# State tiles each with its own place, a joint gate product, and first high halves copied by ScalarE

## The chip, the cores and the metric

One core of a Trainium2 chip runs one step of a hybrid decoder layer. The metric is device time in microseconds (us); lower is better. PE is TensorE (matmuls), DVE is VectorE (elementwise work), ACT is ScalarE (activations and copies), SP is SyncE. DMAs are issued here from SP's queue and, in a few places, from ACT's. All five run at once and meet only at semaphores. The program is a sequence of blocks; every block ends with a barrier of all engines.

## The reference, cut to what matters

```python
xn = rmsnorm(h, norm1)                       # 256 prompt tokens and 8x4 sample tokens, 1024 wide
mq, mk, mv, mo, mi, mf, aq, ak, av, ga, gb = split_proj(xn, w_in)
# mi, mf: 4 + 4 gate columns (one input and one forget gate per head)
hA, C, n, m = mlstm_branch(mq, mk, mv, mo, mi + b_igate, mf + b_fgate, m_norm, C0, n0, m0)
hB = combine_groups(...)                     # dilated window attention
u = sigmoid(ga) * (hA @ w_pa) + sigmoid(gb) * (hB @ w_pb)
h = h + u @ w_o
h = h + moe(rmsnorm(h, norm2))               # 32 experts, top 4
h = h + (p @ w_ple) * sigmoid(rmsnorm(h, norm3) @ w_ple_gate)
```

For the sample tokens `mlstm_branch` multiplies the queries by a stored state `C0` of 8 sequences, 4 heads, 256x256 numbers: one tile of 1 MB for each sequence. The result is normalised, multiplied by a gate, and `hA` goes on to the product with `w_pa`.

## The kernel before, in words

**Lead-in (lines 352 to 547).** `h` gets the tokens. ACT and DVE work out the norms, PE transposes the normed rows, and DVE writes them with the norm weights into `xT` (8 slices of 128 rows by 288 tokens); each of the six writes adds one to `s_xT`. PE then makes the gate product, 8 slices for the input gates and 8 for the forget gates, 4 rows each (line 393). Meanwhile DVE splits `xT` into a rounded high half `xhi` and a rest `xlo`, and then the first piece of the projection weight into `whi` and `wlo`, whose end raises `s_lo`. PE waits for both (lines 397 and 399) and starts the projection: 42 weight pieces of 1 MB (`CHUNKS`), each multiplied as high x high, high x low and low x high for the prompt tokens, and unsplit for the 32 sample tokens. Four raw pieces (`NR`) are loaded ahead by SP; a load waits until PE has used the piece before it in its place.

**Attention (lines 584 to 891).** Two blocks that the diff does not touch.

**mLSTM block (lines 944 to 1209).** SP loads the state tiles. There are six places, two in `ct2` and four in `zaflat`; tile 6 and tile 7 go into the places of tiles 0 and 1. The order on SP's queue is written out by hand: six tile loads, then the stores of the prompt state `C_p` for four heads, then

```python
for b in range(6, NB):
    sp.wait_ge(s_cq, b - 5)
    sp.wait_ge(s_ct[b % 4], 16)
    sp.dma_start(ct[b], ...)
for i in range(4):
    sp.wait_ge(s_cq, 3 + i)
    sp.dma_start(wa[:, 2 * i:2 * i + 2, :], ...)      # w_pa, over the four places in zaflat
```

where `s_cq` counts the tiles that PE has multiplied, and last the small stores `n_s`, `m_p`, `m_s` and a wait for all stores (lines 970 to 972). PE works through four heads, then multiplies the eight tiles into one bank (line 1051), then transposes the finished prompt heads (line 1063, four groups of four, two banks), then the sample head (line 1068). DVE normalises the sample head when all eight tiles are in (line 1193 to `finish`, line 1124), then writes the four transposed groups into `hAT` (line 1199; `hAT` is `xT`), then scales the sample head with ACT's help (lines 1107, 1109, 1202 to 1205) and writes its transposes (line 1208).

**Merge block (lines 1297 to 1561).** SP loads `w_pb`, router weights and expert biases; ACT's queue loads the eight state tiles a second time, into `ring`. PE makes `hA @ w_pa` (line 1286) and, in between, every third step, a state update product (line 1340). DVE prepares the keys of a tile (line 1469), waits for the tile's load, adds the products (line 1474), and SP stores the tile (line 1309). DVE prepares tile b+1 only after tile b. Then DVE splits the expert biases and multiplies the gates (line 1485); PE's second set of products waits for the first of these. Line 1499 adds the branch output to `h`. After that come the experts (line 1575 on) and the last products.

Of the kernel before, what the change touches and what calls it, by code (L numbers as in the profile page):

```python
# [27 lines left out]
F32 = mybir.dt.float32  # L28
F32R = mybir.dt.float32r
# [109 lines left out]
def lay_out(x):  # L139

    x = {k: np.ascontiguousarray(v) for k, v in x.items()}
    a = {k: x[k] for k in ("x_prompt", "x_sample", "cache_k0", "cache_v0", "cache_k1", "cache_v1", "cache_k2",
                           "cache_v2", "w_in", "w_pa", "w_pb", "w_o", "w1", "w2", "w_ple",
                           "w_ple_gate", "norm_f", "b_router")}
    a["ca_in"], a["cb_in"] = CA, CB
    col = lambda v: v.reshape(-1, P).T
    pairs = lambda v: v.reshape(KT // 2, P, 2).transpose(1, 0, 2).reshape(P, KT)
    a["norm_cols"] = np.concatenate([col(x["norm1"][0]), col(x["m_norm"][0]), pairs(x["norm2"][0]), col(x["norm3"][0]),
                                     col(x["norm2"][0])], 1)
    a["w_gates"] = x["w_in"][0][:, GATE0:GATE0 + 2 * MH].reshape(KT, P, 2 * MH).transpose(1, 0, 2)  # L150
    a["b_gates"] = np.stack([x["b_igate"][0], x["b_fgate"][0]], 1)
    a["b1"] = np.tile(x["b1"].reshape(E, 2, 2, 512).transpose(2, 0, 1, 3).reshape(2 * E, 2 * 512), (2, 1))
    a["b2"] = np.tile(x["b2"].reshape(E, 2, 512).transpose(1, 0, 2).reshape(2 * E, 512), (2, 1))
    a["w_router"] = x["w_router"][0].reshape(KT, P, E).transpose(1, 0, 2)
    a["p_prompt"], a["p_sample"] = x["p_prompt"][0, 0], x["p_sample"][0].reshape(NS, PLE)

    C = x["state_C"][0].transpose(1, 0, 3, 2).reshape(MH, NB, 2, P, MD)
    a["CT"] = C.transpose(3, 0, 1, 2, 4)
    n = x["state_n"][0].transpose(1, 0, 2)
    a["n_rows"] = n.reshape(MH * NB, MD)  # L160
    a["n_tok"] = np.repeat(n.reshape(MH * NB, MD), NT, 0)
    a["m_rows"] = x["state_m"][0].T

# [33 lines left out]
def layer(nc, x_prompt, x_sample, cache_k0, cache_v0, cache_k1, cache_v1, cache_k2, cache_v2, w_in, w_pa, w_pb,  # L197
# [68 lines left out]
    def shift_piece(eng):  # L266
# [36 lines left out]
    wlo = sb(st, "wlo", [P, NW, CHUNK], F32R)  # L303
    xhi = sb(st, "xhi", [P, KT, TOK], F32R)
    xlo = sb(st, "xlo", [P, KT, TOK], F32R)
    wif = sb(st, "wif", [P, KT, 2 * MH])
    bif = sb(st, "bif", [MH, 2])
    xn = zaflat[:, 0:3 * D].rearrange("p (t n) -> p t n", t=3)
# [11 lines left out]
    s_lo, s_free, s_xs = sem(st, "s_wlow"), sem(st, "s_wfree"), sem(st, "s_xsplit")  # L320
    s_small = sem(st, "s_small")
    s_ss, s_ms, s_rt, s_xn, s_tr, s_xT = (sem(st, n) for n in (
        "s_sumsq", "s_meansq", "s_root", "s_xn", "s_xtrans", "s_xT"))
# [28 lines left out]
    with nc.Block() as block:  # L352
# [24 lines left out]
        def _(pe):  # L377
# [12 lines left out]
            pe.wait_ge(s_small, 48)  # L390
            for c in range(2):
                for k in range(KT):
                    last = pe.matmul(psG[0:MH, c, 0:TOK], wif[:, k, c * MH:(c + 1) * MH], xT[:, k, :],
                                     start=(k == 0), stop=(k == KT - 1))
                last.then_inc(s_gp, 1)

            pe.wait_ge(s_xs, 2)
            for n, (i, z0, w, k0, nk) in enumerate(CHUNKS):
# [45 lines left out]
        def _(act):  # L444
            for t in range(3):
# [5 lines left out]
                act.wait_ge(s_ms, t + 1)  # L451
                act.activation(ss[0:R, t:t + 1], ss[0:R, t:t + 1], ACT.Sqrt).then_inc(s_rt, 1)
            def stores():
                nb = 4 + 9
# [30 lines left out]
        def _(dve):  # L485
# [17 lines left out]

            high_x, low_x = split(dve, xT[:, :, :], xhi[:, :, :], xlo[:, :, :])
            dve.wait_ge(s_xT, 6)
            high_x().then_inc(s_xs, 1)
            dve.wait_ge(s_xs, 1)
            low_x().then_inc(s_xs, 1)

            def prepare(n):  # L510
                high_w, low_w = split(dve, wraw[:, n % NR, :], whi[:, n % NW, :], wlo[:, n % NW, :])
                dve.wait_ge(s_w[n % NR], 16 * (n // NR + 1))
                if n >= NW:
                    multiplied(dve, n - NW)
                link(high_w())
                low_w().then_inc(s_lo, 1)
# [19 lines left out]
            for n in range(AHEAD):  # L536
                prepare(n)
            for c in range(2):
                dve.wait_ge(s_gp, c + 1)
                dve.tensor_scalar(grow[:, c, :], psG[0:MH, c, 0:TOK], bif[:, c:c + 1], None, ALU.add)  # L540
            dve.wait_ge(s_c, 16)
# [197 lines left out]
    with nc.Block() as block:  # L739
# [72 lines left out]
        def _(dve):  # L812
# [93 lines left out]
    ct2 = sb(ap, "ct", [P, 2, MH, 2 * MD])  # L906
    ct = [(ct2[:, b % 6] if b % 6 < 2 else zaflat[:, (b - 2) * MH * 2 * MD:(b - 1) * MH * 2 * MD].rearrange("p (h n) -> p h n", h=MH))
          for b in range(NB)]
    sv = sb(ap, "sv", [P, MD + 1])
# [34 lines left out]
    with nc.Block() as block:  # L944
        @block.sync
        def _(sp):
            sp.dma_start(nrow[:, :], n_rows).then_inc(s_ld, 16)
            sp.dma_start(ntok[:, :], n_tok).then_inc(s_ld, 16)
            sp.wait_ge(s_stored, n_stored[0])
            for b in range(6):  # L950
                if b >= 4:
                    sp.wait_ge(s_ct[b % 4], 16)
                sp.dma_start(ct[b], CT[:, :, b].rearrange("p h k v -> p h (k v)")).then_inc(s_ct[b % 4], 16)
            for hd in range(MH):
                sp.wait_ge(s_co, 2 * hd + 2)
                sp.dma_start(C_p[hd].rearrange("(a p) e -> p a e", p=P), cst[:, hd % 2].rearrange("p (a e) -> p a e", a=2)).then_inc(s_cst[hd % 2], 16)
                sp.dma_start(n_p[hd:hd + 1], nst[:, hd % 2]).then_inc(s_cst[hd % 2], 16)
            for b in range(6, NB):
                sp.wait_ge(s_cq, b - 5)
                sp.wait_ge(s_ct[b % 4], 16)  # L960
                sp.dma_start(ct[b], CT[:, :, b].rearrange("p h k v -> p h (k v)")).then_inc(s_ct[b % 4], 16)
            for i in range(4):
                sp.wait_ge(s_cq, 3 + i)
                sp.dma_start(wa[:, 2 * i:2 * i + 2, :],
# [10 lines left out]
        def _(pe):  # L975
# [70 lines left out]
            pe.wait_ge(s_qmm, 3)  # L1046
            for b in range(NB):
                pe.wait_ge(s_ct[b % 4], 16 * (b // 4 + 1))
                for half in range(2):
                    for j in range(MH):  # L1050
                        last = pe.matmul(psN_[32 * j:32 * j + 32, 1, 0:MD], qmm[:, half, b, 32 * j:32 * j + 32],
                                         ct[b][:, j, half * MD:(half + 1) * MD],
                                         start=(b == 0 and half == 0), stop=(b == NB - 1 and half == 1))
                last.then_inc(s_cq, 1)

            pe.wait_ge(s_ha, 8)
            for n in range(4):
                if n >= 2:
                    pe.wait_ge(s_hae, n - 1)
                t, half = n // 2, n % 2  # L1060
                for q in range(4):
                    k = 4 * half + q
                    last = pe.transpose(psTR[:, n % 2, q * P:(q + 1) * P], zm[:, t, 2, k * P:(k + 1) * P], ident)
                last.then_inc(s_hat, 1)
            pe.wait_ge(s_ha, 9)
# [46 lines left out]
        def _(dve):  # L1112
# [78 lines left out]
            link(dve.scalar_tensor_tensor(out=sm1[:, 3:4], in0=sm1[:, 2:3], scalar=SC_(3), in1=psN_[:, 0, MD:MD + 1], op0=ALU.mult, op1=ALU.add))  # L1191
            dve.wait_ge(s_cq, NB)
            link(dve.tensor_scalar(ntok[:, :], psN_[:, 1, 0:MD], SC_(3), None, ALU.mult))
            link(dve.tensor_tensor(ntok[:, :], ntok[:, :], psN_[:, 0, 0:MD], ALU.add))
            finish(ntok[:, :], sm1[:, 3:4], SC_(1), zw[:, 3, :])
            for n in range(4):
                dve.wait_ge(s_hat, n + 1)
                t, half = n // 2, n % 2
                dve.tensor_tensor(hAT[:, 4 * half:4 * half + 4, t * P:(t + 1) * P], psTR[:, n % 2, :].rearrange("p (q n) -> p q n", q=4),
                                  mnc[:, 4 * half:4 * half + 4].unsqueeze(2).to_broadcast([P, 4, P]), ALU.mult).then_inc(s_hae, 1)  # L1200
            dve.wait_ge(s_sq, 9)
            dve.tensor_scalar(ssq[:, 8:9], ssq[:, 8:9], 1.0 / MD, EPS, ALU.mult, ALU.add).then_inc(s_sqd, 1)
# [94 lines left out]
    with nc.Block() as block:  # L1297
        @block.sync
        def _(sp):
            vpb = w_pb[0].rearrange("(k p) n -> p k n", p=P)  # L1300
            sp.dma_start(wb_[:, :, :], vpb[:, 0:3, :]).then_inc(s_wb, 16)
            sp.dma_start(ple1[:, :], vpb[:, 3, :]).then_inc(s_wb, 16)
            sp.dma_start(wr[:, :, :], w_router).then_inc(s_sm, 16)
            sp.dma_start(brb, b_router[0].partition_broadcast(P)).then_inc(s_sm, 16)
# [155 lines left out]
        def _(dve):  # L1460
# [29 lines left out]
            def turned(t):  # L1490
                for half in range(2):
# [3 lines left out]
                                      n2r[:, 4 * half:4 * half + 4].unsqueeze(2).to_broadcast([P, 4, ROWS[t]]), ALU.mult).then_inc(s_x2e, 1)  # L1495

            for t in range(2):
                dve.wait_ge(s_pa, 7 + t)
# [546 lines left out]
```

## Time and profile before

| | |
|---|---|
| time, three runs | 1648.76 us median, 1647.61 to 1649.33 |
| the profiled execution | 1647.51 us, of which 1645.7 us are the span from first to last instruction |
| mean granted clock of TensorE | 0.961 of full |
| PE busy | 1500.4 us (91%) |
| DVE busy | 652.7 us (40%) |
| ACT busy | 212.9 us (13%) |
| DMA | 583.00 MB, mean 354 GB/s |

A timeline row reads: start, length, engine, line, operation, tile written <- tiles read, shapes, count, and in brackets how long the engine stood idle before it and what ended that. PEld is the load of a weight into PE, which runs beside products. Matmuls are pipelined: a row of one can overlap the next. An fp32 matmul shows as two records.

### The profile page before, as it was taken

Reading aid. Unit: us, or ns where it says so; the run is one execution under the profiler, and the core shown is the slowest. Engines: PE = TensorE matmul, PEld = TensorE weight load, DVE = VectorE, ACT = ScalarE, POOL = GpSimd, SP = SyncE. Lnnn points to the kernel's source line nnn. Section 1 sums busy time; section 2 is a strip of 40 time slices with the busy share of each in tenths; the row PEclk is TensorE's granted clock in tenths of the full one; section 3 lists DMA queues with packets and bytes.
Section 4 is the critical chain, followed back from the end, with each engine's and each line's share of the span. In section 5 each row is a group of like instructions: output and inputs, shape, how many; then the busy total and the mean of one; then the engine's idle time right before and its main releaser. Section 6 shows DMA issues by size and latency. Waiting matters only on the chain. (4 is left out here: it accounts for less than half of the span.)

```text
span 1645.7 us, 20148 instructions
## 1 busy us (share of the span) xinstructions
PE 1500.4 (91%) x8077; PEld 713.3 (43%) x8077; DVE 652.7 (40%) x1051; ACT 212.9 (13%) x387; POOL 0.3 (0%) x5
## 2 busy tenths in 40 slices
PE   6999999865686898999999999999999999999977
PEld 4777777651463444333333333333333333333333
DVE  5555565345143614133333333333333333323343
ACT  1111110231020002011110111111011111101122
POOL 0000000000000000000000000000000000000000
PEclk9999999987787998999999999999999999999988
DMA  4888889599656993799999999999999999999950
GB/s 167 303 306 306 307 308 364 240 308 415 260 180 237 399 402 142 309 383 428 428 429 428 428 428 429 428 428 428 429 428 428 428 429 428 428 428 429 428 237 29
DMA packets 70200, 583.00 MB, mean 354 GB/s; under 512 B 6116, under 2 KB 8520, under 8 KB 42376
## 3 DMA queue, kind: packets, MB, share of 16 engines
q1 hardware_dynamic: 63528, 570.90, 85.0%
q10 hardware_dynamic: 6624, 11.41, 1.8%
q8 instruction: 37, 0.61, 0.2%
q14 instruction: 11, 0.09, 0.0%
HBM read 568.62 MB, written 67.80 MB: 387 GB/s over the span
## 5 line engine op out<-in xcount | busy, mean ns | idle before, releaser
L1661 PE MATMUL eG<-ring,hBT 128*64 128x512 f32 x1008 | 262.6, 599 | 2.6 <-DMA ring<-w 2.6
L1661 PE MATMUL eL<-ring,hBT 128*64 128x512 f32 x1008 | 259.0, 592 | 0.0
L1703 PE MATMUL eY<-ring,hBT 128*64 128x512 f32 x1024 | 233.9, 598 | 22.0 <-ACT hBT L1743 22.0
L1812 DVE SCALAR_TENSOR_TENSOR h<-eS,rgg,h 128x512 f32<-128x512 f32 (+1 forms) x192 | 135.0, 743 | 208.8 <-PE eS L1687 205.0
L1785 DVE TENSOR_SCALAR xT<-eG 128x512 f32<-128x512 f32 x32 | 22.1, 692 | 302.6 <-PE eL L1661 302.6
L410 PE MATMUL psT<-whi,xhi 128*128 128x512 f32 x336 | 137.0, 408 | 1.2 <-ACT zg L478 1.2
L1661 PEld LDWEIGHTS eL<-ring,hBT 128*64 128x64 f32 x1008 | 72.4, 137 | 143.9 <-issue 143.9
L410 PE MATMUL psT<-whi,xlo 128*128 128x512 f32 x336 | 132.4, 394 | 0.0
L410 PE MATMUL psT<-wlo,xhi 128*128 128x512 f32 x336 | 132.2, 393 | 0.0
L1703 PEld LDWEIGHTS eY<-ring,hBT 128*64 128x64 f32 x1024 | 67.9, 136 | 144.5 <-issue 114.9
L1661 PEld LDWEIGHTS eG<-ring,hBT 128*64 128x64 f32 x1008 | 66.0, 136 | 130.3 <-issue 119.4
L349 DVE CAST whi<-wraw 128x2048 fp32r<-128x2048 f32 x42 | 51.5, 1226 | 122.4 <-PE psT L414 122.4
L350 DVE TENSOR_TENSOR wlo<-wraw,whi 128x2048 fp32r<-128x2048 f32 x42 | 96.3, 2292 | 1.4
L1637 PE MATMUL eA<-zg,selU 128*64 128x512 f32 x396 | 90.6, 592 | 1.7 <-DVE selU L1774 1.7
L1752 ACT ACTIVATE xT<-xT 128x512 f32<-128x512 f32 x32 | 20.2, 630 | 468.3 <-DVE xT L1785 468.3
L410 PEld LDWEIGHTS psT<-whi,xhi 128*128 128x128 f32 x336 | 63.0, 188 | 27.5 <-issue 14.7
L1687 PE MATMUL eS<-yS,selT 128*128 128x512 f32 x192 | 71.5, 452 | 3.7 <-DVE yS L1798 2.7
L410 PEld LDWEIGHTS psT<-whi,xlo 128*128 128x128 f32 x336 | 63.1, 188 | 15.1
L410 PEld LDWEIGHTS psT<-wlo,xhi 128*128 128x128 f32 x336 | 63.2, 188 | 13.1
L1687 PEld LDWEIGHTS eS<-yS,selT 128*128 128x128 f32 x192 | 29.0, 189 | 81.2 <-issue 75.5
L1286 PE MATMUL pX<-za,xT 128*128 128x512 f32 x128 | 61.4, 632 | 2.6 <-PEq L944 2.6
L1637 PEld LDWEIGHTS eA<-zg,selU 128*64 128x64 f32 x396 | 28.4, 137 | 58.1 <-issue 56.0
(411 smaller groups left out, 1279.3 us busy)
## 6 DMA issues: line engine op xcount, KB each, us to landing
ring<-w SPq DMA_DIRECT2D x190, 2048.0 KB, 19.3
wraw<-w_in SPq DMA_DIRECT2D x42, 1024.0 KB, 7.2
k_s<-cache_k SPq DMA_DIRECT2D x8, 2040.0 KB, 10.4
v_s<-cache_v SPq DMA_DIRECT2D x8, 2040.0 KB, 31.6
ring<-CT ACTq DMA_DIRECT2D x8, 1024.0 KB, 17.9
C_s<-ring SPq DMA_DIRECT2D x8, 1024.0 KB, 10.7
k_s<-cache_k SPq DMA_DIRECT2D x4, 2032.0 KB, 9.9
v_s<-cache_v SPq DMA_DIRECT2D x4, 2032.0 KB, 9.9
```

The source lines that it names most:

```text
L349: return (lambda: dve.tensor_copy(high, raw), lambda: dve.tensor_tensor(low, raw, high.bitcast(F32), ALU.subtract))
L350: lambda: dve.tensor_tensor(low, raw, high.bitcast(F32), ALU.subtract))
L410: last = pe.matmul(ps[:, c, :], a[:, k0 + k, t * P:(t + 1) * P], b[:, k, c * 512:(c + 1) * 512], start=(k0 + k == 0 and a is xh and b is w ...
L1286: last = pe.matmul(pX[t][:, c, :], xt[:, k, t * P:(t + 1) * P], wts[k][:, c * 512:(c + 1) * 512], start=(k == 0), stop=(k == kt - 1))
L1637: last = pe.matmul(pA[64 * c:64 * c + 64, :], selU[:, t, 0:CAP], x2[:, t, c * 512:(c + 1) * 512], start=(t == 0), stop=(t == 2))
L1661: last = pe.matmul(ps[64 * hh:64 * hh + 64, :], xgT[:, k % 4, (k // 4) * CAP:(k // 4 + 1) * CAP], src[:, c, col:col + 512], start=False, s ...
L1687: pe.matmul(pSc[c][:, :], selT[:, t * P:(t + 1) * P], yS[:, c, :], start=True, stop=True).then_inc(S["sc"], 1)
L1703: last = pe.matmul(pY[64 * hh:64 * hh + 64, :], acT[:, k % 4, (k // 4) * CAP:(k // 4 + 1) * CAP], ring[:, c, col:col + 512], start=False, ...
L1752: act.activation(sg, glu, ACT.Sigmoid, scale=ALPHA).then_inc(S["sg"], 1)
L1785: dve.tensor_scalar(glu, pG[:, :], LIMIT, None, ALU.min).then_inc(S["glu"], 1)
L1812: dve.scalar_tensor_tensor(out=x, in0=pSc[c][0:R, :], scalar=rgg[0:R, t:t + 1], in1=x, op0=ALU.mult, op1=ALU.add).then_inc(S["acc"], 1)
```

## The change

Three things are changed.

The lead-in: the input gate's 4 columns and the forget gate's 4 columns are laid out in one weight of 36 columns (4, 28 zeros, 4), so that one product of 8 slices gives both, in rows 0 to 3 and 32 to 35 of one bank. ACT copies the first weight piece's high half and, in two pieces of 128 tokens, the high half of `xT`; DVE makes the rests, also in two pieces, for the 256 prompt tokens alone. PE waits for four of these steps.

The mLSTM block: all eight state tiles have a place of their own. Tile 6 lies in `xT` and tile 7 in `h`. They are loaded and multiplied in the order `CQ`, the four of `zaflat` first; no tile load waits for PE any more. The `w_pa` loads wait for the first to the fourth tile multiplied. PE transposes the prompt heads in two parts between the tiles, after the fifth and after the seventh, and DVE writes them out before it normalises the sample head.

The merge block: `h` is loaded again from `x_prompt` (two loads of 512 KB on SP's queue, behind `w_pb`), and DVE waits for it before line 1499.

```diff
-    a["w_gates"] = x["w_in"][0][:, GATE0:GATE0 + 2 * MH].reshape(KT, P, 2 * MH).transpose(1, 0, 2)
+    wg = x["w_in"][0][:, GATE0:GATE0 + 2 * MH].reshape(KT, P, 2 * MH).transpose(1, 0, 2)
+    a["w_gates"] = np.concatenate([wg[:, :, 0:MH], np.zeros((P, KT, 32 - MH), np.float32), wg[:, :, MH:2 * MH]], 2)
...
-    xhi = sb(st, "xhi", [P, KT, TOK], F32R)
-    xlo = sb(st, "xlo", [P, KT, TOK], F32R)
+    xhi = sb(st, "xhi", [P, KT, SEQ], F32R)
+    xlo = sb(st, "xlo", [P, KT, SEQ], F32R)
+    GC = 32 + MH
...
-            for c in range(2):
-                for k in range(KT):
-                    last = pe.matmul(psG[0:MH, c, 0:TOK], wif[:, k, c * MH:(c + 1) * MH], xT[:, k, :],
-                                     start=(k == 0), stop=(k == KT - 1))
-                last.then_inc(s_gp, 1)
-
-            pe.wait_ge(s_xs, 2)
+            for k in range(KT):
+                last = pe.matmul(psG[0:GC, 0, 0:TOK], wif[:, k, :], xT[:, k, :], start=(k == 0), stop=(k == KT - 1))
+            last.then_inc(s_gp, 1)
+
+            pe.wait_ge(s_xs, 4)
...
+            act.wait_ge(s_w[0], 16)
+            act.activation(whi[:, 0, :], wraw[:, 0, :], ACT.Copy).then_inc(s_whi0, 1)
+            for t in range(2):
+                act.wait_ge(s_xT, 2 * t + 2)
+                act.activation(xhi[:, :, t * P:(t + 1) * P], xT[:, :, t * P:(t + 1) * P], ACT.Copy).then_inc(s_xs, 1)
...
-            high_x, low_x = split(dve, xT[:, :, :], xhi[:, :, :], xlo[:, :, :])
-            dve.wait_ge(s_xT, 6)
-            high_x().then_inc(s_xs, 1)
-            dve.wait_ge(s_xs, 1)
-            low_x().then_inc(s_xs, 1)
+            dve.wait_ge(s_xs, 2)
+            for t in range(2):
+                a = slice(t * P, (t + 1) * P)
+                dve.tensor_tensor(xlo[:, :, a], xT[:, :, a], xhi[:, :, a].bitcast(F32), ALU.subtract).then_inc(s_xs, 1)
...
-                link(high_w())
+                if n:
+                    link(high_w())
+                else:
+                    dve.wait_ge(s_whi0, 1)
                 low_w().then_inc(s_lo, 1)
...
+    ct = ([ct2[:, 0], ct2[:, 1]]
+          + [state_rows(zaflat[:, i * MH * 2 * MD:(i + 1) * MH * 2 * MD]) for i in range(4)]
+          + [state_rows(xT[:, :, :].rearrange("p k n -> p (k n)")[:, 0:MH * 2 * MD]),
+             state_rows(h[:, 0:2, :].rearrange("p t n -> p (t n)"))])
+    CQ = (2, 3, 4, 5, 6, 0, 1, 7)
...
-            for b in range(6):
-                if b >= 4:
-                    sp.wait_ge(s_ct[b % 4], 16)
-                sp.dma_start(ct[b], CT[:, :, b].rearrange("p h k v -> p h (k v)")).then_inc(s_ct[b % 4], 16)
+            for i, b in enumerate(CQ):
+                if i >= 4:
+                    sp.wait_ge(s_ct[i % 4], 16)
+                sp.dma_start(ct[b], CT[:, :, b].rearrange("p h k v -> p h (k v)")).then_inc(s_ct[i % 4], 16)
...
-            for b in range(6, NB):
-                sp.wait_ge(s_cq, b - 5)
-                sp.wait_ge(s_ct[b % 4], 16)
-                sp.dma_start(ct[b], CT[:, :, b].rearrange("p h k v -> p h (k v)")).then_inc(s_ct[b % 4], 16)
             for i in range(4):
-                sp.wait_ge(s_cq, 3 + i)
+                sp.wait_ge(s_cq, 1 + i)
...
+            def ha_trans(t):
+                pe.wait_ge(s_ha, 8)
+                for half in range(2):
+                    if t:
+                        pe.wait_ge(s_hae, half + 1)
+                    for q in range(4):
+                        k = 4 * half + q
+                        last = pe.transpose(psTR[:, half, q * P:(q + 1) * P], zm[:, t, 2, k * P:(k + 1) * P], ident)
+                    last.then_inc(s_hat, 1)
+
+            for i, b in enumerate(CQ):
+                pe.wait_ge(s_ct[i % 4], 16 * (i // 4 + 1))
...
                 last.then_inc(s_cq, 1)
-
-            pe.wait_ge(s_ha, 8)
-            for n in range(4):
...
+                if b in (6, 1):
+                    ha_trans(0 if b == 6 else 1)
...
-            dve.wait_ge(s_cq, NB)
-            link(dve.tensor_scalar(ntok[:, :], psN_[:, 1, 0:MD], SC_(3), None, ALU.mult))
-            link(dve.tensor_tensor(ntok[:, :], ntok[:, :], psN_[:, 0, 0:MD], ALU.add))
-            finish(ntok[:, :], sm1[:, 3:4], SC_(1), zw[:, 3, :])
+            dve.wait_ge(s_cq, 5)
             for n in range(4):
                 dve.wait_ge(s_hat, n + 1)
...
+            dve.wait_ge(s_cq, NB)
+            link(dve.tensor_scalar(ntok[:, :], psN_[:, 1, 0:MD], SC_(3), None, ALU.mult))
+            link(dve.tensor_tensor(ntok[:, :], ntok[:, :], psN_[:, 0, 0:MD], ALU.add))
+            finish(ntok[:, :], sm1[:, 3:4], SC_(1), zw[:, 3, :])
...
             sp.dma_start(ple1[:, :], vpb[:, 3, :]).then_inc(s_wb, 16)
+            for t in range(2):
+                sp.dma_start(h[:, t, :], x_prompt[0, t * P:(t + 1) * P]).then_inc(s_hload, 16)
             sp.dma_start(wr[:, :, :], w_router).then_inc(s_sm, 16)
...
+            dve.wait_ge(s_hload, 80)
             for t in range(2):
                 dve.wait_ge(s_pa, 7 + t)
```

## Rows read from the trace of the kernel before

**Rows 1.** The page's slices: busy tenths of PE and of DMA in 40 parts.
```profile
PE   6999999865686898999999999999999999999977
...
DMA  4888889599656993799999999999999999999950
```

**Rows 2.** Timeline of the lead-in, SP's queue, PE and DVE.
```profile
4.02 38.04 SPq L366 DMA_DIRECT2D wraw<-w_in  x6
...
17.88 10.22 PE L393 MATMUL psG<-xT,wif 128*4 128x288 f32 x32 [0.38 <-DVE xT L499]
...
19.25 2.56 DVE L350 TENSOR_TENSOR xlo<-xT,xhi 128x2304 fp32r<-128x2304 f32 x1
...
22.60 0.09 PEld L393 LDWEIGHTS psG<-xT,wif 128*4 128x4 f32 x1 [0.32 <-issue]
...
22.98 2.29 DVE L350 TENSOR_TENSOR wlo<-wraw,whi 128x2048 fp32r<-128x2048 f32 x1
...
27.45 0.09 PEld L393 LDWEIGHTS psG<-xT,wif 128*4 128x4 f32 x1 [0.16 <-issue]
...
28.03 0.50 PE L410 MATMUL psT<-whi,xhi 128*128 128x512 f32 x1
```

**Rows 3.** Timeline of ACT: its first work after the norms.
```profile
51.43 1.03 ACT L478 ACTIVATE zm<-psT 128x1024 f32<-128x1024 f32 x1 [39.00 <-PE psT L410]
```

**Rows 4.** The five weight loads of line 366 that start before 40 us.
```profile
DMA to landing us min/median/max: 4.9/8.6/12.7
```

**Rows 5.** Timeline of PE: state tiles, head transposes, start of the merge block.
```profile
500.65 3.46 PE L1051 MATMUL mN<-ct,qmm 128*32 128x256 f32 x28
...
503.95 3.83 PE L1051 MATMUL mN<-za,qmm 128*32 128x256 f32 x61
...
513.13 1.07 PE L1051 MATMUL mN<-ct,qmm 128*32 128x256 f32 x16 [3.07 <-DMA ct<-CT]
514.13 1.97 PE L1063 MATMUL mTR<-ca,zm 128*128 128x128 f32 x8
...
523.99 7.24 PE L1286 MATMUL pX<-za,xT 128*128 128x512 f32 x12 [2.57 <-PEq L944]
```

**Rows 6.** Timeline of DVE: the sample head and the block's last write.
```profile
514.34 0.48 DVE L1193 TENSOR_SCALAR ntok<-mN,colsb 128x256 f32<-128x256 f32 x1 [9.90 <-PE mN L1051]
...
519.71 0.14 DVE L1202 TENSOR_SCALAR ssq<-ssq 128x1 f32<-128x1 f32 x1
...
521.24 0.51 DVE L1208 TENSOR_TENSOR xT<-mTR,cols 128x128 f32<-128x128 f32 x2 [0.57 <-PE mTR L1068]
```

**Rows 7.** Timeline of ACT beside them: the end of the sample head's square.
```profile
516.79 0.19 ACT L1107 ACTIVATION_READ_ACCUMULATOR scr<-zw 128x1 f32 x1
```

**Rows 8.** Timeline of SP's queue: the two late tile loads.
```profile
503.06 1.89 SPq L961 DMA_DIRECT2D ct<-CT  x2
```

**Rows 9.** SP's waits: total us, times, longest.
```profile
SPq L972 <- DMA m_s<-mnew: 13.2, 1, 13.2
```

**Rows 10.** Windows: PE, PEld, DVE, ACT, POOL busy, granted clock, DMA share, GB/s.
```profile
516.00:518.00 2.00, 1.00 (x5) 0.91 (x5) 1.64 (x3) 0.51 (x2) 0.00 (x0) 0.50 1.04 424
...
540.00:542.00 2.00, 2.00 (x10) 0.83 (x5) 1.19 (x2) 0.00 (x0) 0.00 (x0) 0.50 1.05 389
```

**Rows 11.** Timeline of DVE in the merge block.
```profile
535.59 1.41 DVE L1474 SCALAR_TENSOR_TENSOR ring<-ring,za,pT_ 128x512 f32<-128x512 f32 x2 [11.25 <-DMA ring<-CT]
...
568.59 1.41 DVE L1474 SCALAR_TENSOR_TENSOR ring<-ring,za,pT_ 128x512 f32<-128x512 f32 x2 [1.80 <-DMA ring<-CT]
...
574.39 2.36 DVE L1485 TENSOR_TENSOR zg<-pX,zg 128x1024 f32<-128x1024 f32 x2
```

**Rows 12.** Timeline of PE in the merge block.
```profile
538.63 0.80 PE L1340 MATMUL pT_<-za,ring 32*128 32x256 f32 x2 [3.54 <-DVE ring L1469]
...
540.68 4.87 PE L1286 MATMUL pX<-za,xT 128*128 128x512 f32 x6
...
576.03 2.84 PE L1286 MATMUL pX<-wb,hBT 128*128 128x512 f32 x6
```

More of the change, by code:

```diff
@@ L149, in lay_out @@
                                      col(x["norm2"][0])], 1)
-    a["w_gates"] = x["w_in"][0][:, GATE0:GATE0 + 2 * MH].reshape(KT, P, 2 * MH).transpose(1, 0, 2)
-    a["b_gates"] = np.stack([x["b_igate"][0], x["b_fgate"][0]], 1)
+    wg = x["w_in"][0][:, GATE0:GATE0 + 2 * MH].reshape(KT, P, 2 * MH).transpose(1, 0, 2)
+    a["w_gates"] = np.concatenate([wg[:, :, 0:MH], np.zeros((P, KT, 32 - MH), np.float32), wg[:, :, MH:2 * MH]], 2)
+    a["b_gates"] = np.concatenate([x["b_igate"][0], np.zeros(32 - MH, np.float32), x["b_fgate"][0]])[:, None]
     a["b1"] = np.tile(x["b1"].reshape(E, 2, 2, 512).transpose(2, 0, 1, 3).reshape(2 * E, 2 * 512), (2, 1))
@@ L303, in layer @@
     wlo = sb(st, "wlo", [P, NW, CHUNK], F32R)
-    xhi = sb(st, "xhi", [P, KT, TOK], F32R)
-    xlo = sb(st, "xlo", [P, KT, TOK], F32R)
-    wif = sb(st, "wif", [P, KT, 2 * MH])
-    bif = sb(st, "bif", [MH, 2])
+    xhi = sb(st, "xhi", [P, KT, SEQ], F32R)
+    xlo = sb(st, "xlo", [P, KT, SEQ], F32R)
+    GC = 32 + MH
+    wif = zaw[:, :, :].rearrange("p a b -> p (a b)")[:, 0:KT * GC].rearrange("p (k c) -> p k c", k=KT)
+    bif = sb(st, "bif", [GC, 1])
     xn = zaflat[:, 0:3 * D].rearrange("p (t n) -> p t n", t=3)
@@ L321, in layer @@
     s_small = sem(st, "s_small")
+    s_whi0 = sem(st, "s_whi_first")
     s_ss, s_ms, s_rt, s_xn, s_tr, s_xT = (sem(st, n) for n in (
@@ L537, in _ @@
                 prepare(n)
+            dve.wait_ge(s_gp, 1)
             for c in range(2):
-                dve.wait_ge(s_gp, c + 1)
-                dve.tensor_scalar(grow[:, c, :], psG[0:MH, c, 0:TOK], bif[:, c:c + 1], None, ALU.add)
+                dve.tensor_scalar(grow[:, c, :], psG[32 * c:32 * c + MH, 0, 0:TOK], bif[32 * c:32 * c + MH, :], None, ALU.add)
             dve.wait_ge(s_c, 16)
@@ L906, in layer @@
     ct2 = sb(ap, "ct", [P, 2, MH, 2 * MD])
-    ct = [(ct2[:, b % 6] if b % 6 < 2 else zaflat[:, (b - 2) * MH * 2 * MD:(b - 1) * MH * 2 * MD].rearrange("p (h n) -> p h n", h=MH))
-          for b in range(NB)]
+    state_rows = lambda x: x.rearrange("p (h n) -> p h n", h=MH)
+    ct = ([ct2[:, 0], ct2[:, 1]]
[3 more added lines that the diff above has]
+    CQ = (2, 3, 4, 5, 6, 0, 1, 7)
     sv = sb(ap, "sv", [P, MD + 1])
@@ L1046, in _ @@
             pe.wait_ge(s_qmm, 3)
-            for b in range(NB):
-                pe.wait_ge(s_ct[b % 4], 16 * (b // 4 + 1))
+            def ha_trans(t):
[9 more added lines that the diff above has]
+                pe.wait_ge(s_ct[i % 4], 16 * (i // 4 + 1))
                 for half in range(2):
@@ L1052, in _ @@
                                          ct[b][:, j, half * MD:(half + 1) * MD],
-                                         start=(b == 0 and half == 0), stop=(b == NB - 1 and half == 1))
+                                         start=(i == 0 and half == 0), stop=(i == NB - 1 and half == 1))
                 last.then_inc(s_cq, 1)
-            pe.wait_ge(s_ha, 8)
-            for n in range(4):
[L1058 to L1064, printed above, removed]
+                if b in (6, 1):
+                    ha_trans(0 if b == 6 else 1)
             pe.wait_ge(s_ha, 9)
```

## The prediction

> **What bounds the kernel now.** First the page's slices: PE is at 9 tenths nearly everywhere, and the dips lie in slice 0, in slices 8 to 13 (counted from 0) and at the end [rows 1]. So a gain must come from a place where PE waits or does needless work on the path. The change touches three. The timeline of the lead-in shows that the projection starts at 28.03, directly behind the last gate record at 27.45, while DVE had finished its part at 22.98 + 2.29 = 25.27 [rows 2]: the gate product sets that start, DVE has 2.8 us in hand. In the mLSTM block the timeline of PE shows the eighth tile delayed by 3.07 us by its load, and behind it a row of steps, PE to DVE to ACT and back, up to DVE's write at 521.24 + 0.51 = 521.75 [rows 5, 6]. Yet the next block starts only at 523.99 [rows 5]: SP's waits show 13.2 us for the last small store [rows 9], which stands behind 4 MB of w_pa on SP's queue. So two things end that block almost together, the engines first, SP last. In the merge block DMA is at 9 (slice 13, from 535) [rows 1], and the DVE timeline has two waits for tile loads, 11.25 us for the first and 1.80 us for the last [rows 11].
>
> **Lead-in.** Removed: 8 of 16 gate matmuls, 16 of 32 records. The start of the last 21 records is spaced (27.45 - 22.60)/20 = 0.24 us; the eleven before them take (22.60 - 17.88)/11 = 0.43 each, about twice as long [rows 2]. The new product has the same 288 moving columns, so I take the same time for a record, and 36 instead of 4 weight columns at nothing, as PEld runs beside PE. If the spacing changes at the same time as before, the last of 16 records starts at 22.60 + 4 x 0.24 = 23.57, and with the 0.58 us from the last record to the first projection matmul the projection starts at 24.15: 3.9 us earlier. If all 16 kept the slow spacing: 17.88 + 15 x 0.43 + 0.58 = 24.9, a gain of 3.1.
>
> Does the other input come in time? ACT has stood idle since 51.43 - 39.00 = 12.43 [rows 3]. Weight piece 0 is first of four on one queue, so its load takes no longer than the median 8.6 us of [rows 4], and it was issued at 4.02 [rows 2]: there by 12.6. ACT needs 1.03 us for 1024 elements [rows 3], so about 2.1 for the piece, done by 14.7, and twice 1.03 for xhi. The second of these waits only for the fourth write of xT, which lies before the sixth at about 17.85 (the gate product starts on it), so xhi is complete by 18.9 at the latest. DVE then makes xlo, 2.56 x 2048/2304 = 2.3, plus some 0.1 for the second instruction, and wlo, 2.29 [rows 2]: 23.6 at the latest. That is still 0.5 before 24.15. If the cover failed, each us that ACT is later costs one. Gone from DVE are 1.36 us of xhi and 1.2 of the first high half, both of which were hidden. The most to be had is where DVE sets the start, 17.9 + 2.3 + 2.3 = 22.5, and the gate records are all fast: a gain of 5.2 with a margin for the waits. I take 3.9. The projection after it runs on PE alone (its slices are at 8 and 9), so this passes on whole. The gate additions on DVE, two as before, and the second piece's split stand behind it with a whole piece on PE to hide in.
>
> **mLSTM block.** The tile loads: eight are issued in one run, at the pace of landing, while PE is at the heads; 2 MB more in a stretch whose DMA slice, 11, stands at 5 [rows 1]. I cost them at nothing: PE's heads hide them, and the two last have no wait for PE any more. They go past the four C_p stores on SP's queue; the store of head 0 can be held until the fourth tile has landed, and ACT needs its buffer back only two heads later. If that cover failed, ACT would stand.
>
> On PE the first 32 records (two tiles) ran until 503.95, and the next 64, four tiles, took 3.83 us or 0.96 each [rows 5]. Five tiles then end at 503.95 + 2.87 = 506.8; the first eight head transposes took 1.97, and the window behind them has a granted clock of 0.50, 1.2 GHz [rows 5, 10]; I take half of 1.97, 1.0, because they now follow tiles at the faster pace without a wait: 507.8; two tiles, 509.7; eight transposes, 510.7; the last tile, 1.07: 511.8, where it was 514.2. DVE's four writes of hAT fall between the tiles (PE needs the first two of them 1.9 us after it made their input). The sample head starts 0.14 after the last tile as before: 511.95. To the end of ACT's square with its accumulator it is 516.79 + 0.19 - 514.34 = 2.64 [rows 6, 7]; line 1202, which stood behind the four writes until 519.71, can then follow 0.05 later, and from its start to the last write it is 521.75 - 519.71 = 2.04 [rows 6]. End of the engines: 511.95 + 2.64 + 0.05 + 2.04 = 516.7, 5.1 us earlier.
>
> SP, which was later, must gain too. Before, its queue moved 2 tiles and w_pa, 6.3 MB, from 503.06 [rows 8]; at 424 GB/s [rows 10] that is 14.8 us, and SP was free at about 523.5: 5.6 us went for the start, gaps and the last store's return. Now w_pa alone, 4.2 MB or 9.9 us, is issued from the end of the first tile, about 502.2. With the same 5.6 SP is free at 517.7; if the gaps came from the tile loads, nearer 516. So the block ends between 516.7 and 517.7, and the next starts 0.5 after, between 517.2 and 518.2: 5.8 to 6.8 us earlier. I take 6.3.
>
> **Merge block.** Added: 1.05 MB for h, at 389 to 424 GB/s 2.5 to 2.7 us of all DMA engines, in a stretch whose DMA is full [rows 1, 10]. Who waits? The last tile's load already holds DVE by 1.80, its four additions, two of them 1.41, end near 571.3, the biases follow, the gate product starts at 574.39 and ends its first half at 575.6, and PE's second set of products starts at 576.03 on it [rows 11, 12]. So about 0.4 us of delay is hidden and the rest passes on. From below the cost is nothing (if ACT's queue keeps its share of the engines while SP's is only longer), from above 2.7. The DVE's wait for the last tile shows that its landing counts, so I go above the middle: a delay of 2.1, a cost of 1.7. The wait on h itself (line 1499) comes only after the products with w_o and costs nothing.
>
> The page "DMA: Bandwidth & Descriptors" of the Trainium skill, section "Queues, rings and completion order", says that each DMA engine takes turns between the queues that have work, a packet at a time; that the first tile took over 11 us agrees with shared engines. By that rule the loads of h also slow the first tiles, and the sum would be that of the third rival below.
>
> Sum: 3.9 + 6.3 - 1.7 = 8.5 us. The profiled execution took 1647.51, so 1639.0; the median of the three runs stands 1.25 above it, so **1640.3** for the median. About 0.2%, 3.3 us, is what can be told from no change.
>
> **Rivals.** (1) SP's stores still set the end of the mLSTM block: w_pa lands no faster, for instance because it is held by its own gates, and only 503.06 - 502.2 = 0.9 is won there. For it: SP was last before. Against: a third of the bytes ahead of it are gone. 3.9 + 0.9 - 1.7 = 3.1: 1645.7.
>
> (2) The lead-in gains nothing, as ACT's chain replaces the gate product: then 4.6 in all, 1644.2. It takes a weight piece that lands after about 16, against the bound of 12.6.
>
> (3) h delays the first tile too, by its full 2.5, and PE's wait of 3.54 grows by that; six products behind a wait took 4.87 where they take 2.84 later [rows 12]; one more such round is 2.0. 3.9 + 6.3 - 4.5 = 5.7: 1643.1. Against: the first tile landed while SP's queue still held other loads, so it may not feel a longer queue.
>
> (4) Slower: the clock. After that wait of 3.54 the granted clock was again 0.50 [rows 10], and the six products of a round cost 4.87 - 2.84 = 2.0 us more; its state product took 540.68 - 538.63 = 2.05, and if that is halved at full clock the round costs 3.0 more. If late tiles bring PE into such a wait in every round, the block loses up to 7 x 3.0 = 21 us; from the fourth round on (10.2/3.0 = 3.4) the gain is gone. At five rounds: 1648.76 - 10.2 + 15.0 = 1653.6. Against it: a slow round lasts longer than the loads of a tile, so the loads catch up and the waits end. The page "TensorE: Matmul & The Clock Gate", section "HAM oscillation — how this bites in real kernels", of the Trainium skill tells of just that, a PE put back to the low clock by each wait for a load; the row after the wait agrees once.
>
> **How the numbers follow.** The forecast has 0.70, (1) 0.06, (2) 0.05, (3) 0.15, (4) 0.04. The forecast's own range: gains of 3.1 + 5.8 - 2.7 = 6.2 to 5.2 + 6.8 - 0 = 12.0, so 1636.8 to 1642.6, and the runs spread about 0.9 to either side. The range takes in (3) and (2): 1636.0 to 1645.0. Faster: the forecast, (2) and (3), 0.90; the same: (1), 0.06; slower: (4), 0.04.
>
> **What would show it.** Right: 16 records of line 393, the first projection matmul near 24.2 behind a gate record; the eighth tile without a wait for a load, the merge block's start some 10 us earlier than 523.99 on the profile's clock (3.9 + 6.3); a longer DVE wait at line 1474. Wrong: a projection start released by DVE or ACT; SP in line 972 well after DVE's last write; PE waits of several us in more than two rounds; or a wait for hload.

## The result and the profile after

The changed kernel took 1637.03 us (median of four runs, 1636.32 to 1639.47) where the kernel before took 1648.18 beside it: a ratio of 0.9936, 95% interval 0.9912 to 0.996, so 6.6 to 14.5 us less. The forecast was 1640.3 in a range of 1636.0 to 1645.0. The profiled execution took 1636.94 us, 1635.2 of them the span, at a mean granted clock of 0.965.

The timeline of the lead-in (start, length, engine, line, operation) answers to [rows 2, 3]:

```profile
12.54 1.89 ACT L455 ACTIVATE whi<-wraw 128x2048 fp32r<-128x2048 f32 x1
...
14.82 1.06 ACT L458 ACTIVATE xhi<-xT 128x1024 fp32r<-128x1024 f32 x1 [0.39 <-DVE xT L506]
...
17.04 1.06 ACT L458 ACTIVATE xhi<-xT 128x1024 fp32r<-128x1024 f32 x1 [1.16 <-DVE xT L506]
...
18.08 6.25 PE L395 MATMUL psG<-xT,zaw 128*36 128x288 f32 x16 [0.39 <-DVE xT L506]
18.13 2.36 DVE L514 TENSOR_TENSOR xlo<-xT,xhi 128x1024 fp32r<-128x1024 f32 x2
20.41 2.28 DVE L353 TENSOR_TENSOR wlo<-wraw,whi 128x2048 fp32r<-128x2048 f32 x1
24.26 0.50 PE L411 MATMUL psT<-whi,xhi 128*128 128x512 f32 x1
```

There are 16 gate records instead of 32, and DVE is done at 20.41 + 2.28 = 22.69, 1.6 us before the projection starts. So the gate product still sets that start. From the first gate record to the first projection matmul it is 24.26 - 18.08 = 6.18 us, where it was 28.03 - 17.88 = 10.15 [rows 2]: 4.0 us gained.

The mLSTM block's end, in the timelines of PE and DVE and the waits of SP, answers to [rows 5, 6, 9]. PE:

```profile
494.12 0.65 PE L1070 MATMUL mN<-za,qmm 128*32 128x256 f32 x3
...
500.38 1.09 PE L1063 MATMUL mTR<-ca,zm 128*128 128x128 f32 x8
501.40 1.93 PE L1070 MATMUL mN<-ct,qmm 128*32 128x256 f32 x32
503.26 1.09 PE L1063 MATMUL mTR<-ca,zm 128*128 128x128 f32 x8
504.28 1.07 PE L1070 MATMUL mN<-h,qmm 128*32 128x256 f32 x16
509.13 0.44 PE L1079 MATMUL mTR<-ca,zw 128*128 128x128 f32 x2 [3.77 <-DVE zw L1217]
511.90 1.19 PE L1298 MATMUL pX<-za,xT 128*128 128x512 f32 x1 [2.33 <-PEq L957]
```

DVE, and SP's waits (total us, times, longest):

```profile
509.50 0.49 DVE L1220 TENSOR_TENSOR xT<-mTR,cols 128x128 f32<-128x128 f32 x2 [0.42 <-PE mTR L1079]
511.90 0.35 DVE L1483 TENSOR_SCALAR ring<-za 128x256 f32<-128x256 f32 x1 [1.92 <-PEq L957]
525.32 1.41 DVE L1488 SCALAR_TENSOR_TENSOR ring<-ring,za,pT_ 128x512 f32<-128x512 f32 x2 [13.06 <-DMA ring<-CT]
```
```profile
SPq L981 <- DMA m_s<-mnew: 10.0, 1, 10.0
```

No tile waits for a load any more. From the first state product to the merge block's first product it is 511.90 - 494.12 = 17.78 us. Before, the first state product was this row of PE's timeline, the first of the 32 records of [rows 5]:

```profile
500.23 0.65 PE L1051 MATMUL mN<-ct,qmm 128*32 128x256 f32 x3
```

So it was 523.99 - 500.23 = 23.76: 6.0 gained. The engines finish at 509.50 + 0.49 = 509.99, the barrier opens 1.9 later, and SP is the one that is late: it has waited 10.0 us for its last small store.

The DVE row at 525.32 answers to [rows 11]: the wait for the first tile of the merge block has grown from 11.25 to 13.06. The eighth tile, in the same timeline:

```profile
559.68 1.41 DVE L1488 SCALAR_TENSOR_TENSOR ring<-ring,za,pT_ 128x512 f32<-128x512 f32 x2 [2.15 <-DMA ring<-CT]
```

Its additions start 559.68 - 511.90 = 47.78 us after the block's start, when its load has landed; before it was 568.59 - 523.99 = 44.60, on the load too [rows 11]. PE's timeline there answers to [rows 12]:

```profile
511.90 8.15 PE L1298 MATMUL pX<-za,xT 128*128 128x512 f32 x12 [2.33 <-PEq L957]
...
528.36 0.81 PE L1354 MATMUL pT_<-za,ring 32*128 32x256 f32 x2 [4.44 <-DVE ring L1483]
...
530.40 4.88 PE L1298 MATMUL pX<-za,xT 128*128 128x512 f32 x6
...
536.30 2.84 PE L1298 MATMUL pX<-za,xT 128*128 128x512 f32 x6
...
566.77 2.84 PE L1298 MATMUL pX<-wb,hBT 128*128 128x512 f32 x6
```

PE's wait is 4.44 instead of 3.54, one round runs slowly (4.88 for six products) and the next is at 2.84 again. From the block's start to the second set of products it is 566.77 - 511.90 = 54.87 us, where it was 576.03 - 523.99 = 52.04: 2.8 lost.

That makes 4.0 + 6.0 - 2.8 = 7.2 us, less than the timed difference of 10.5. One more gain is in a place that the prediction passed over. PE's timeline at the first matmul of the third and of the 35th weight piece, first before, then after:

```profile
41.56 0.50 PE L410 MATMUL psT<-whi,xhi 128*128 128x512 f32 x1
...
258.42 0.50 PE L410 MATMUL psT<-whi,xhi 128*128 128x512 f32 x1
```
```profile
37.63 0.50 PE L411 MATMUL psT<-whi,xhi 128*128 128x512 f32 x1
...
251.69 0.50 PE L411 MATMUL psT<-whi,xhi 128*128 128x512 f32 x1
```

The same 32 pieces take 216.86 us before and 214.06 after. PE waits for nobody in either; each matmul simply starts 0.227 us (median) after the one before it instead of 0.232. Over all 42 pieces that would be 2.80 x 42/32 = 3.7 us, an estimate from these 32.

### The profile page after: what moved, and what is told of

The parts are those of the page before. It is cut to its first block and busy times, and to the rows that moved or that the text cites. A ratio compares the mean times of both kernels' runs of the same rounds, so it can differ in the third digit from the quotient of the medians.

```text
span 1635.2 us, 20121 instructions
## 1 busy us (share of the span) xinstructions
PE 1488.8 (91%) x8061; PEld 710.5 (43%) x8061; DVE 650.2 (40%) x1050; ACT 216.8 (13%) x390; POOL 0.3 (0%) x5
```

## The experiments

The table has for each kernel the time, and four intervals of its profile in us. **Lead-in**: first gate record to first projection matmul. **32 pieces**: start of the third to start of the 35th weight piece. **Block**: first state product to the merge block's first product. **Merge**: from there to the second set of products. Each ratio is to runs of the kernel before made beside that kernel, with medians from 1647.55 to 1648.64.

| kernel | median us | ratio to before (95%) | lead-in | 32 pieces | block | merge |
|---|---|---|---|---|---|---|
| before | 1648.18 | | 10.15 | 216.86 | 23.76 | 52.04 |
| changed | 1637.03 | 0.9936 (0.9912 to 0.996) | 6.18 | 214.06 | 17.78 | 54.87 |
| lead-in alone | 1638.96 | 0.9947 (0.9932 to 0.9962) | 6.39 | 214.06 | 23.98 | 52.25 |
| places alone | 1645.67 | 0.9985 (0.9969 to 1.0001) | 10.09 | 216.86 | 17.73 | 54.91 |
| transposes last | 1634.81 | 0.9929 (0.991 to 0.9949) | 6.73 | 214.06 | 17.72 | 55.84 |
| h after w_o | 1632.02 | 0.9906 (0.9891 to 0.9921) | 6.97 | 214.06 | 17.57 | 52.08 |
| 256 in before | 1646.40 | 0.9985 (0.9968 to 1.0002) | 10.43 | 214.06 | 23.65 | 52.29 |
| 288 in changed | 1638.26 | 0.9939 (0.9921 to 0.9957) | 6.50 | 216.86 | 17.32 | 56.14 |
| 256, shifted | 1642.91, one run | | 9.50 | 217.43 | 23.37 | 52.01 |
| highs by DVE | 1635.92 | 0.9925 (0.9902 to 0.9949) | 7.28 | 214.06 | 18.33 | 55.84 |
| gates twice | 1645.03, one run | | 10.52 | 214.06 | 17.70 | 56.53 |
| w_pa gates as before | 1637.49 | 0.993 (0.9905 to 0.9955) | 6.29 | 214.06 | 19.03 | 55.43 |
| small stores by ACT | 1635.44 | 0.9925 (0.9905 to 0.9946) | 5.54 | 214.06 | 18.10 | 53.38 |
| h late, stores by ACT | 1631.89 | 0.9903 (0.9884 to 0.9923) | 6.40 | 214.06 | 16.80 | 51.12 |

The time of a kernel scatters by some us from run to run, and so do stages that no edit touches. The column of 32 pieces repeats to 0.01 us; the block and the merge column fall into groups that don't overlap, with and without the edit in question. So verdicts on a step are taken from the columns.

**The two halves of the change, each alone.** The lead-in hunks of the diff alone:

> Only the lead-in part of the change. Theory A (each part acts in its own stage): the projection starts 3.8 us earlier, as in the changed kernel (24.26 against 28.03), and the whole gains 3.8, with every later stage as long as before. Rival B (part of the 10.6 us between the two profiled spans was set free in the untouched stages by the earlier start): the sample attention, too, is shorter by more than 1 us and the whole gains over 5.

The mLSTM and merge hunks alone:

> Only the mLSTM and merge parts of the change. Theory A: from the first state product to the start of the merge block 6.0 us less, from there to the second products 2.8 more, 3.2 gained in all; lead-in at 28.03. Rival B (the gain is one chain, each part works only with the other): well under 2 us, or over 5.

The lead-in alone is worth 6.3 to 11.2 us by the clock, its start 10.15 - 6.39 = 3.8: this run first showed that it holds something more. The places alone gain 6.0 in the block and lose 2.9 behind it. Neither half needs the other.

**The h loads at another place.**

```diff
             sp.dma_start(ple1[:, :], vpb[:, 3, :]).then_inc(s_wb, 16)
-            for t in range(2):
-                sp.dma_start(h[:, t, :], x_prompt[0, t * P:(t + 1) * P]).then_inc(s_hload, 16)
...
             sp.dma_start(wa, w_o[0].rearrange("(k p) n -> p k n", p=P)).then_inc(s_wa, 16)
+            for t in range(2):
+                sp.dma_start(h[:, t, :], x_prompt[0, t * P:(t + 1) * P]).then_inc(s_hload, 16)
```

> The changed kernel with the two loads of h moved on SP's queue to behind the load of w_o, where h is needed only at line 1514. Theory A (the loads of h cost the merge block its 2.8 us): the first state tile lands some 11.6 us after the block's start as before, the merge stage is as long as before the change, and the whole gains 13 us over the kernel before, 2.8 more than the changed kernel. Rival B (the merge block is longer because it starts with another clock and another queue state): the first tile still lands after 13 us, no gain over the changed kernel.

DVE's wait for the first tile, in its timeline:

```profile
524.33 1.41 DVE L1488 SCALAR_TENSOR_TENSOR ring<-ring,za,pT_ 128x512 f32<-128x512 f32 x2 [11.79 <-DMA ring<-CT]
```

The wait falls from 13.06 to 11.79 and the merge column is back at 52.08. In eight profiles with h ahead of the router weights this column is 53.4 to 56.5, in the six others 51.1 to 52.3. So those two loads cost 2.8 us in this pair, 1.1 to 5.4 over the profiles, and nothing in this block where they stand behind w_o.

**The head transposes back at the end**, on PE and on DVE, with the new places kept:

```diff
-                if b in (6, 1):
-                    ha_trans(0 if b == 6 else 1)
+            ha_trans(0)
+            ha_trans(1)
```

> The changed kernel with the prompt heads' transposes again behind all tiles and DVE's writes behind the sample head. Theory A (SP's last store, behind w_pa, ends the mLSTM block, and the engines have 1.4 us in hand): the engines end some 1 us later than now, the merge block starts within 0.7 us of where it does now, relative to the first state product (17.8). Rival B (the new order of the transposes is what shortens the block): the merge block starts 2 to 3 us later.

The block takes 17.72 us, as with the moved transposes. DVE's last write ends 506.70 - 490.30 = 16.40 us after the first state product instead of 509.99 - 494.12 = 15.87: the moved transposes shorten the engines' work by 0.5, but in both kernels the engines are done before the block ends.

**What ends the block.** First the w_pa loads with their old gates, then the small stores (of n_s, shown here, m_p and m_s) on another queue:

```diff
-                sp.wait_ge(s_cq, 1 + i)
+                sp.wait_ge(s_cq, 3 + i)
```

> The changed kernel, with the four loads of w_pa waiting for the third to the sixth multiplied tile as before, instead of the first to the fourth; nothing else differs. Theory (the block ends when w_pa, behind fewer other bytes, has landed, and the earlier issue is part of the gain): w_pa is issued two tiles, about 2 us, later and the next block starts about 2 us later: first state product to merge start 19.5 to 20 us instead of 17.8. Rival (tile loads out of the way are the whole gain; the gates matter nothing since the queue is still busy with other loads): 17.8 to 18.2.

```diff
-            store(sp, n_s, nrow[:, :])
...
             act.wait_ge(s_nno, 1)
+            act.dma_start(n_s, nrow[:, :]).then_inc(s_stored, 16)
             act.wait_ge(s_hh, 2 * MH + 1)
```

> The changed kernel, with the three small stores at the end of the mLSTM block issued from ACT's queue, so that they no longer stand behind the loads of w_pa on SP's. Theory of the prediction's first rival (the last small store on SP's queue sets the block's end): the engines are done at 509.99, the last load of w_pa lands near 511.2; first state product to merge start falls from 17.78 to about 16.5, as far as the engines allow, and the time by about 1.2 us. Theory that w_pa's own landing sets it: the barrier falls earlier, but PE's first product then waits for w_pa, and the merge start moves by 0.6 us at most.

SP's queue, with the new gates and with the old:

```profile
496.95 3.07 SPq L973 DMA_DIRECT2D za<-w_pa  x4
```
```profile
498.16 4.10 SPq L973 DMA_DIRECT2D za<-w_pa  x4
```

With the old gates w_pa is issued 498.16 - 492.97 = 5.2 us after the first state product instead of 496.95 - 494.12 = 2.8, and the block takes 19.03, 1.25 longer. So 1.25 of the 6.0 comes from the earlier issue in this pair (the other kernels with the new places and gates take 16.80 to 18.33), less than the 2 expected; the last load lands 9.4 us after its issue instead of 11.5. In the kernel before, w_pa was issued 505.27 - 500.23 = 5.0 us after the first state product, at nearly the same place as with the old gates here; its last load landed 523.30 - 500.23 = 23.1 us after it, and here 511.25 - 492.97 = 18.3. These 4.8 us go with the two tile loads, which stood ahead of w_pa on the queue.

With the stores moved to ACT's queue, the barrier opens 0.3 us after DVE's last write, but PE now stands for w_pa, in the timelines of DVE and PE:

```profile
511.16 0.51 DVE L1221 TENSOR_TENSOR xT<-mTR,cols 128x128 f32<-128x128 f32 x2 [0.57 <-PE mTR L1076]
512.00 0.35 DVE L1484 TENSOR_SCALAR ring<-za 128x256 f32<-128x256 f32 x1 [0.33 <-PEq L957]
```
```profile
510.65 0.69 PE L1076 MATMUL mTR<-ca,zw 128*128 128x128 f32 x2 [3.77 <-DVE zw L1218]
513.39 8.36 PE L1299 MATMUL pX<-za,xT 128*128 128x512 f32 x12 [2.05 <-DMA za<-w_pa]
```

The block took 18.10 (16.80 in the last experiment, where PE waits for w_pa too), so what is late is the landing of w_pa itself. The small stores only stood behind it: in this run the block is no shorter with them moved.

**The address of the weights.** xhi and xlo are the 128x128 weights of the projection matmuls. In the changed kernel their rows lie 256 columns apart, before 288. Each layout in the other kernel; in the one of before, within the same room, so that no other tile moves (xhi is shown, xlo is alike):

```diff
-    xhi = sb(st, "xhi", [P, KT, TOK], F32R)
+    xhi = sb(st, "xhi", [P, KT * TOK], F32R)[:, 0:KT * SEQ].rearrange("p (k n) -> p k n", k=KT)
```

> The kernel before, with only the rows of xhi and xlo laid 256 columns apart instead of 288, in the same room, so that no other tile moves; DVE splits the 256 prompt tokens alone. Theory (the row pitch of the weights sets the spacing of the projection matmuls): spacing 0.2275 us instead of 0.232, a projection piece of 48 matmuls 13.4 us instead of 13.55, about 3.5 us less in all over 42 pieces; the projection's start stays near 28.0, since the gate product sets it; ratio about 0.998. Rival (the spacing comes from the place of other tiles, or from ACT and DVE working less beside PE in the lead-in): spacing as before, ratio 1.000.

> The changed kernel, with xhi and xlo laid out 288 columns apart again, the last 32 unused. Theory (row pitch): spacing 0.232 us again, the projection 3 to 3.5 us longer, start of the projection still near 24.3; about 1640 us where the changed kernel took 1637. Rival (place of other tiles): spacing stays 0.2275 and the time at 1637.

(The "piece of 48 matmuls" of these texts is two weight pieces of 24.) The column that matters, 32 pieces, changes sides both times, to 0.01 us: 214.06 with 256 columns, 216.86 with 288, whatever else the kernel does. By the clock the first gains 2.5 us (from 5.3 gained to 0.3 lost), which fits 3.7 but would not have shown it. The second took 1638.26, 1.2 above the changed kernel and less than the 3.7 that the column says, which tells nothing by itself. Then the 256-column rows moved 32 columns on:

> The kernel before, with the rows of xhi and xlo 256 columns apart, as in the run that changed this alone, but both moved 32 columns (128 bytes) on in their room. If the distance between rows sets the spacing of the projection matmuls, it stays at 0.2275 us and a piece of 48 at 13.4 us. If the address of a row does (at 288 columns most rows begin at an odd multiple of 128 bytes), every row is now off and the spacing goes back to 0.232 us, 13.55 us a piece, or is higher.

PE's timeline at the same two matmuls:

```profile
41.17 0.50 PE L410 MATMUL psT<-whi,xhi 128*128 128x512 f32 x1
...
258.60 0.50 PE L410 MATMUL psT<-whi,xhi 128*128 128x512 f32 x1
```

217.43 us, slower than with 288 columns. My first theory, the distance between rows, falls: the distance is still 256. It is where a row begins. With all rows 128 bytes further on, 32 pieces take 3.37 us more. (With 288 columns a row begins 9 x 128 bytes behind the one before, so of eight rows four, and not most, lie an odd number of 128 bytes from the first; the cost of 2.80 is well over half of 3.37.)

**The parts of the lead-in.** ACT's copies given back to DVE with the joint product kept, and the joint product made twice with the copies kept:

```diff
+                dve.tensor_copy(xhi[:, :, a], xT[:, :, a]).then_inc(s_xs, 1)
...
-                if n:
-                    link(high_w())
-                else:
-                    dve.wait_ge(s_whi0, 1)
+                link(high_w())
```

> The changed kernel, with the one gate product kept and ACT's three copies of high halves given back to DVE. The prediction's row sums: DVE then makes xhi (about 1.2 us more), xlo, the first whi (1.2) and wlo one after another behind the sixth write of xT at about 17.9: done by 25.1 instead of 22.7, so DVE and not the gate product sets the projection's start, near 25.5 instead of 24.3; ACT's copies are worth about 1.2 us of the 3.8 on top of the gate product. Rival (ACT's copies are worth nothing, the gate product alone decides): start stays at 24.3. Second rival (they carry most of it): start near 28.

```diff
-            for k in range(KT):
-                last = pe.matmul(psG[0:GC, 0, 0:TOK], wif[:, k, :], xT[:, k, :], start=(k == 0), stop=(k == KT - 1))
+            for c in range(2):
+                for k in range(KT):
+                    last = pe.matmul(psG[0:GC, c, 0:TOK], wif[:, k, :], xT[:, k, :], start=(k == 0), stop=(k == KT - 1))
```

> The changed kernel, with the joint gate product of 36 rows made twice, so that PE has as many records as before; ACT's copies are kept. By the prediction (the gate product sets the start, ACT's copies alone give nothing): the projection starts again at 28 or a little later, since 36 columns are loaded instead of 4. Rival (ACT's copies carry the gain): start stays near 24.3 to 25.

Without the copies DVE sets the start, in the timeline:

```profile
22.86 2.29 DVE L353 TENSOR_TENSOR wlo<-wraw,whi 128x2048 fp32r<-128x2048 f32 x1
...
25.30 0.47 PE L411 MATMUL psT<-whi,xhi 128*128 128x512 f32 x1 [0.47 <-DVE wlo L353]
```

The column says 7.28 us instead of 6.18, where the eight kernels with both edits scatter from 5.5 to 7.0; in the run's own profile PE has stood idle for 0.47 before that product. With the product twice it is 10.52, a little above the kernel before. So the joint product carries the gain; on top of it the copies are worth 0.5 to 1.1, and without it nothing.

**The best of these.** h behind w_o and the small stores by ACT:

> The changed kernel with what the earlier runs point to: the two loads of h stand behind w_o on SP's queue, and the three small stores are issued from ACT's. By the stage table: 2.8 us less in the merge block (52.1 instead of 54.9), 0.6 to 1.2 us less at the end of the mLSTM block; together 3.4 to 4 us below the changed kernel, about 1633 us, ratio to before 0.991.

1631.89 us, against about 1633 expected. The two kernels with h behind w_o have the lowest ratios, 0.9906 and 0.9903, and the first differs from the changed kernel by the h loads alone; that the stores add anything is not shown. Against the changed kernel's 0.9936 the intervals still touch (0.9923 above, 0.9912 below); what carries the claim is the merge column, 51.1 and 52.1 against 54.9.

## Why the prediction came out as it did

**Lead-in: right.** Forecast 3.9, measured 4.0. The product still sets the start, DVE comes in 1.6 us before it, and the copies are needed for that, as the run without them shows (DVE last, start at 25.30). The second rival is out.

**"The projection after it runs on PE alone, so this passes on whole": incomplete.** It passed on, but the same diff moved the weights of 1008 matmuls to other addresses, and I costed that at nothing without a word. It is worth 2.80 us over 32 pieces, an estimated 3.7 in all. No row of before could have priced it: only one spacing stood there. In the profiled pair nearly all of it is hidden: from its first matmul to the end of its last product the projection takes 285.81 us before and 285.57 after. Near its end PE waits for ACT, first before, then after:

```profile
286.72 0.47 PE L410 MATMUL psT<-whi,xhi 128*128 128x512 f32 x1 [1.16 <-ACT zg L478]
```
```profile
281.38 0.47 PE L411 MATMUL psT<-whi,xhi 128*128 128x512 f32 x1 [2.84 <-ACT zg L485]
```

Behind the wait of 1.16 the granted clock stays at 1.00 (286 to 290); behind the one of 2.84 it is 0.50, 1.2 GHz, from 282 to 284. So 1.7 of the 3.7 went into the longer wait and, an estimate by difference, some 1.8 into products at the low clock. The run of the places alone, which has the same lead-in and projection as before, has a wait of 2.89 and a clock of 0.50 behind it (290 to 292), and its projection is 289.07 - 285.57 = 3.5 longer than the changed kernel's. Why this wait differs from one profile to the next is open.

**mLSTM block: the size right, the reason half right.** Forecast 17.0 to 18.0 us from the first state product to the merge block's start, measured 17.78; forecast gain 6.3, measured 6.0. The text let the engines or SP end the block, at 516.7 or 517.7. It is SP, by more than a us: w_pa lands late, and what makes it earlier than before is that no tile load stands ahead of it on the queue, with 1.25 of the 6.0 from the earlier gates. The engines had to be earlier too, but not by so much: their last write came 521.75 - 500.23 = 21.52 us after the first state product before and comes 15.87 after it now, 5.65 less (forecast 5.1). At 21.52 they would have held the block; the 0.5 that the moved transposes give are worth nothing. The first rival put SP last, which is so, but gave it a gain of 0.9; it was 6.0.

**Merge block: the path right, the delay too small.** Forecast cost 1.7, measured 2.8. The prediction let the landing of the last tile count, and that is what ends the stretch: in all fourteen profiles DVE's wait for the eighth tile ends on its load. It took a delay of 2.1 there, of which 0.4 would be hidden. The eighth tile's additions start 47.78 - 44.60 = 3.2 us later, above even the 2.7 that it allowed, and from there to the second set of products it is 7.09 where it was 7.44, so 0.35 is hidden. The term that failed is the delay of 2.1. Why it is 3.2 here and not 2.7 is open; over the profiles the eighth tile starts 44.0 to 45.0 us into the block without h ahead of it, and 46.3 to 49.4 with h.

The third rival was right that the first tile is late too, by 1.8 us; the argument against it, that the first tile landed while SP's queue held other loads, failed. But its way from there, a PE wait longer by 2.5 and one more slow round, did not come about: the wait grew by 0.9, and there is one slow round of 4.88, as before. The fourth rival did not come about either. The Trainium skill, "DMA: Bandwidth & Descriptors", section "Queues, rings and completion order", says that each DMA engine takes turns between the queues that it has work for. The first tile agrees with that: loads on SP's queue delayed a load on ACT's, 13.06 against 11.79.

**The sum.** 4.0 + 6.0 - 2.8 + 3.7 = 10.9, and the timed difference is 10.5 (6.6 to 14.5). The forecast 8.5 was low since the missed 3.7 outweighs the two terms that came out lower, by 0.3 and 1.1; that the time came within 3.3 us of the forecast is in part luck, as these errors have opposite signs. Without the change of address the kernel would by the column stand near 1641, and the run of it took 1638.26; both lie inside the range.

The agreement of 10.9 with 10.5 proves little. In the profiled pair, where the projection gained only 0.24, the spans still differ by 10.5, and 3.4 of that lies where the diff shortens nothing: 2.1 between the projection's end and the first state product, and 1.3 behind the second set of products. These two stretches vary by 6.5 and 4.4 us over the fourteen profiles.

## What to carry to other kernels

When a diff changes a tile's shape or place, list every instruction that reads it, also where its count and shape stay the same, and look at the spacing of those instructions in a long undisturbed run of them: it repeats to 0.01 us where whole times scatter by several. When a block ends with a barrier, list the arrivals in order: moving the last arrival forward gains only as far as the next one, and work taken off an engine that already waits there is worth nothing. A load put on a busy stretch belongs behind the loads that somebody is waiting for, on every queue that shares the DMA engines.

## What was not expected of the hardware

The spacing of a matmul stream depended on where its weights lie in the row of a partition: 32 pieces (768 matmuls of 512 columns, and the sample tokens' products) took 214.06 us with rows of 1024 bytes, 217.43 with the same rows 128 bytes further on, and 216.86 with rows of 1152 bytes. In the shifted layout the starts of most matmuls are alternately about 0.229 and 0.237 us apart; in the first layout most are 0.226 or 0.227 apart. Which multiple of an address counts, whether it counts by itself or against the address of whi and wlo, and whether the moved xhi or the moved xlo does it, was not tried.
